# One VectorE addition placed ahead of a subtraction in the second feed-forward, and the second head's activation moved from the mixer's start to its second unit

## The reference

```python
# mixer: one head after the other (8 heads, key width 128)
f = lbf + (1.0 - lbf) * jax.nn.sigmoid(f_logit.astype(f32))
k = 1.0 - f
logf = jnp.log(f)
qf = jax.nn.silu(q.astype(f32))
...
ac = jnp.cumsum(to_chunks(logf, A_KDIM), axis=3)
# per chunk: scores from q, k and exp of differences of ac, then the output and the state S
...
# feed-forward
u, v = jnp.split(z @ w_up[l], 2, axis=-1)
u = causal_dwconv(u, conv_w[l], conv_b[l])
h = h + (jax.nn.silu(u) * v) @ w_down[l]
```

## Time and profile before

| | us |
|---|---|
| median of 3 runs | 3150.68 |
| lowest and highest | 3145.3, 3151.42 |
| the profiled execution | 3153.7 |
| its span, first to last instruction | 3151.9 |
| second mixer, slots 0 to 31 | 1563 to 2165 |
| second feed-forward, turns with down sums | 2486 to 3056 |

### The profile page before, as it was taken

How to read it: one execution, slowest core, us unless ns; L and a number is a source line. 1 busy time by engine, 2 the same in 40 slices (tenths; PEclk the granted TensorE clock), 3 DMA queues, 4 the chain that set the end, 5 groups by cost and what they waited for, 6 DMA issues and landing times. The chain is left out here.

```text
span 3151.9 us, 52430 instructions
## 1 busy us (share of the span) xinstructions
PE 3046.3 (97%) x22212; PEld 2640.2 (84%) x22212; DVE 1520.4 (48%) x2121; ACT 1044.3 (33%) x1503; POOL 751.7 (24%) x634
## 2 busy tenths in 40 slices
PE   7999999799999999999999999999999999999999
PEld 6778888678788888888998999898978888888887
DVE  6898664543433333446365656663432333333333
ACT  3133444333212222133445555554322112111112
POOL 0003321312211222121243434432221122221121
PEclk9999999899999999999999999999999999999999
DMA  3111000311111111123111010112421111111111
GB/s 120 49 47 28 3 3 3 139 63 61 61 40 40 47 47 47 61 81 103 41 48 48 28 48 28 48 46 97 134 97 41 61 47 47 47 57 43 40 41 74
DMA packets 198609, 173.28 MB, mean 55 GB/s; under 512 B 8829, under 2 KB 180437, under 8 KB 198037
## 3 DMA queue, kind: packets, MB, share of 16 engines
q1 hardware_dynamic: 191509, 162.01, 16.2%
q10 hardware_dynamic: 6912, 8.52, 0.8%
HBM read 149.41 MB, written 21.10 MB: 54 GB/s over the span
## 5 line engine op out<-in xcount | busy, mean ns | idle before, releaser
L2142 POOL TENSOR_TENSOR ffn_w_lo<-ffn_raw,ffn_w_hi 128x1024 fp32r<-128x1024 f32 x86 | 207.1, 2409 | 1052.8 <-ACT ffn_w_hi L2302 794.6
L2163 PE MATMUL ffn_out<-blk_hi,ffn_w_hi 128*128 128x512 f32 (+1 forms) x1584 | 446.1, 369 | 3.9 <-DVE blk_lo L1948 2.5
L2163 PE MATMUL ffn_out<-blk_hi,ffn_w_lo 128*128 128x512 f32 (+1 forms) x1584 | 445.6, 369 | 0.0
L2163 PE MATMUL ffn_out<-blk_lo,ffn_w_hi 128*128 128x512 f32 (+1 forms) x1584 | 445.1, 369 | 0.0
L3223 PE MATMUL mix_e<-blk_hi,mix_w_hi 128*128 128x348 f32 (+1 forms) x1056 | 349.0, 331 | 5.6 <-DVE blk_lo L2421 2.9
L3223 PE MATMUL mix_e<-blk_lo,mix_w_hi 128*128 128x348 f32 (+1 forms) x1056 | 342.0, 324 | 0.0
L3223 PE MATMUL mix_e<-blk_hi,mix_w_lo 128*128 128x348 f32 (+1 forms) x1056 | 341.0, 323 | 0.0
L2163 PEld LDWEIGHTS ffn_out<-blk_hi,ffn_w_hi 128*128 128x128 f32 x1584 | 288.7, 189 | 49.5 <-issue 4.9
L2163 PEld LDWEIGHTS ffn_out<-blk_lo,ffn_w_hi 128*128 128x128 f32 x1584 | 288.7, 189 | 44.0
L2163 PEld LDWEIGHTS ffn_out<-blk_hi,ffn_w_lo 128*128 128x128 f32 x1584 | 288.3, 189 | 44.4
L2302 ACT ACTIVATE ffn_w_hi<-ffn_raw 128x1024 fp32r<-128x1024 f32 x44 | 46.7, 1061 | 740.5 <-PE ffn_out L2163 740.5
(11 more groups left out here) (387 smaller groups left out, 5419.1 us busy)
## 6 DMA issues: line engine op xcount, KB each, us to landing
ffn_raw<-ffn_up SPq DMA_DIRECT2D x44, 512.0 KB, 3.8
mix_raw<-w_in SPq DMA_DIRECT2D x44, 512.0 KB, 3.8
ffn_raw<-w_up SPq DMA_DIRECT2D x44, 512.0 KB, 3.8
ffn_d_raw<-ffn_down SPq DMA_DIRECT2D x11, 1024.0 KB, 5.7
ffn_d_raw<-w_down SPq DMA_DIRECT2D x11, 1024.0 KB, 5.8
proj_w_raw<-w_in_first SPq DMA_DIRECT2D x19, 512.0 KB, 3.8
branch_gates<-proj SPq DMA_DIRECT2D x16, 520.0 KB, 4.7
wout_raw<-w_out SPq DMA_DIRECT2D x16, 512.0 KB, 4.2
```

The source lines that it names most:

```text
L2142: G.by(nc.gpsimd.tensor_tensor(w_lo[i % 2][:], raw[i % 2][:], w_hi[i % 2][:], ALU.subtract), f"lo{i}")
L2163: mm = nc.tensor.matmul(o, a[i % 2][:, k, :], b[:, k, first:first + n], start=k == 0 and part == 0, stop=k == KD - 1 and part == 2)
```

## The change

In the second feed-forward, DVE's addition of down0 (`drain(0, 1)`) is placed between `hidden(1)` and `hidden_lo(1)`; the other fifteen stay behind `hidden_lo(1)`. The list of names is changed to the same order. In the mixer, `activate_head(1)` is taken from ahead of slot 0 and put into slot 1, after the last exponentials of unit 2 and before the evacuation of dense piece 32. No instruction is added or removed, apart from register work. Lines of the changed kernel are shifted by 2 or 3.

```diff
--- before.py
+++ after.py
@@ -2013,7 +2013,9 @@
                 dve_names += [f"tapa{2 * q + e}", f"tapb{2 * q + e}"]
         dve_names += [f"hid{q}", f"hid_lo{q}"]
     dve_names += DOWN
-    if not second:
+    if second:
+        dve_names = dve_names[:dve_names.index("hid_lo1")] + ["down0", "hid_lo1"] + DOWN[1:]
+    else:
         dve_names = dve_names[:dve_names.index("tapa3")] + ["tapa3", "down0", "tapb3", "down1", "down2", "hid1", "down3",
                                                             "down4", "hid_lo1"] + DOWN[5:]
     pe_names = [f"up{i}" for i in range(4)] + DOWN
@@ -2475,8 +2477,9 @@
                 if second:
                     taps_of(1)
                     hidden(1)
+                    drain(0, 1)
                     hidden_lo(1)
-                    drain(0, 2 * NT)
+                    drain(1, 2 * NT)
                     return
                 A.wait(dve, g, "y2")
                 tap(2, 1, taps + wide, "tapa2")
@@ -2966,7 +2969,6 @@
             evacuate(25)
             last_level(0)
             evacuate(26)
-            activate_head(1)
             for u in range(slots):
                 more, dense, tiles = u + 1 < slots, pieces_of_slot(u), tiles_of(u)
                 if more:
@@ -2994,6 +2996,8 @@
                     last_level(u + 1)
                 if u and u % 8 == 0:
                     deviation(u // 8 - 1)
+                if u == 1:
+                    activate_head(1)
                 activations(u)
                 for p in dense[2:]:
                     evacuate(p)
```

## The result

| | before | changed |
|---|---|---|
| median (runs) | 3149.22 us (4) | 3127.48 us (4) |
| lowest and highest | 3145.3, 3151.42 | 3124.0, 3132.04 |
| the profiled execution, its span | 3153.7, 3151.9 | 3132.04, 3130.2 |

The ratio of changed to before is 0.9931, with a 95% interval of 0.9919 to 0.9942: 21.7 us less, and between 18.3 and 25.5 by the interval. The forecast was 3131.7 us, 19.0 less, with a range of 3124.5 to 3141.

A forecast was written before the change was run, and what follows sets the result against it. PE, busy 97%, bounds the kernel, so only its waits can be won. Feed-forward 12.2 plus slot 0's 7.2 minus 0.4 in slot 2 gives 19.0 us less: 3131.7 us, 80% range 3124.5 to 3141.

The forecast's parts named there:

- What bounds the kernel: Whole kernel: PE is busy 97% of the span, so time can only be won where PE stands still.
- The moved addition: Second feed-forward, DVE: down0's addition fills the hole before the low part, about 2487.5 to 2488.2, with 0.35 us to spare.
- the choice between 12.2 and 5.6 us: Second feed-forward, nine turns: 12.2 us gained if POOL doesn't hold the moved addition; 5.6 if it does, a rival at 8%.
- Down3 and down4: Second feed-forward: down3's stall of 1.46 us goes, down4 keeps a 0.11 us restart; 1.35 us gained a turn, 12.2 in nine.
- The tie at down4: Second feed-forward: down1's addition ends at 2491.36, down4 is due at 2491.42; no time waited, but a 0.11 us restart probably stays.
- Slot 0: Mixer: the 3.57 us wait vanishes, the keys wait some 0.3, keys to scores take 4.44; 7.2 us gained, lower bound 4.7.
- Slots 1 and 2: Mixer: the block in slot 1 makes ACT 0.9 us late against 0.6 slack in slot 2; PE loses 0.4 us once.
- The rival of a delay that is carried: Mixer, 2%: slot 2 doesn't absorb ACT's delay and 30 later slots wait; 0.9 us costs 12 us, 1.5 gives 3162.
- the rival of a longer switch of tables: Slot 1, 3%: ACT empties 1.28 us before each of two loads, block 7.4 us, PE waits 2.6 more; gain 16.4, 3134.
- The sum: Whole kernel: 12.2 + 7.2 - 0.4 = 19.0 us less, 3131.7 us against the median; the forecast has 73%.
- The clock at slots 8, 16 and 24: Mixer: some 3 us of the range allowed for the clock's fall appearing or vanishing there and for the spread of runs.

The follow-up runs named there:

- Both halves alone: Against the kernel before: only the feed-forward's addition moved, 3139.02 us, ratio 0.996; only head 1's activation moved to slot 1, 3143.56 us, ratio 0.998.
- the longer block: Changed kernel with two more table loads and two 472-column activations ahead of head 1's activation in slot 1: 3136.21 us, ratio 0.996 to the kernel before.
- the repeated pair: Changed kernel and kernel before, both unchanged, once more on another chip: 3129.98 us (ratio 0.9938) and 3151.01 us (ratio 1.0001).
- the experiments for 0.3 and 1 us: Changed kernel with head 1's activation at slot 0's end, 3129.44 us; with two additions ahead of the low part, 3128.44 us; with three, 3130.01 us.

## Why the prediction was right

1. **What bounds the kernel.** PE, and what counts is its idle places and the lower clock behind them. Both halves alone gave what they took out of PE's chain.
2. **The moved addition.** Forecast to start directly behind the gating, to take 0.69 us, and to leave 0.35 us before the low part; the trace has 0.69 and 0.34. That POOL doesn't hold it, the choice between 12.2 and 5.6 us, was right. The Trainium skill (GPSIMD Engine Reference, Specifications) names a collision for VectorE instructions with two SBUF inputs (and for those in a two-port mode, which no run here shows); the trace agrees, 0.69 us for the addition with an operand in PSUM and for the low part 2.21 us beside POOL, 1.26 with an overlap of 0.17 us and 1.22 behind POOL.
3. **Down3 and down4.** The tie at down4 came as forecast, with the restart of 0.11 us and no bracket, and the late weight load shows the reason that the prediction gave. The chain has the sixteen sums in 21.93 us; from the first down matmul to the next up product it was 2509.24 - 2485.92 = 23.32 before and is 2498.52 - 2476.59 = 21.93 now. 1.39 us in this turn and 12.4 in the nine together, for 1.35 and 12.2.
4. **Slot 0.** 7.3 us for 7.2. The keys' wait is 0.36 for 0.3, keys to scores 4.43 for 4.44. One step in it was right with too weak a proof: that PE is at the values at 1567.69 doesn't show dense piece 27 finished when its evacuation was to start, at 1566.95. The trace of before does. Piece 27's last matmul ends at 1566.52:

```profile
1566.20 0.32 PE L3223 MATMUL mix_e<-blk_hi,mix_w_lo 128*128 128x348 f32 x1
```

   More than half of the gain is the idle time of 3.57 and part of the 1.55; (13.25 - 5.94) - (3.57 + 1.55 - 0.36) = 2.6 us of it is matmuls that no longer run at the lower clock, and a restart saved.
5. **Slots 1 and 2.** 0.26 us for 0.4, and some luck in it. The delay was 0.62 us and not 0.9: the block started 0.12 us earlier against the scores of slot 1 and took 4.74 us in place of 4.86. The slack was smaller too. The prediction counted 0.6 us from the end of DVE's sum to the outputs, but PE starts them 0.25 to 0.26 us behind that end even when it is waiting, as here and with the longer block, so about 0.35 were free. The two errors nearly cancel, and the restart of 0.11 us isn't seen here. The loss vanishes in the trace with the block at the end of slot 0, and it is paid once, as the longer block shows with sixteen times the loss (4.11 us over 1.33, for 0.26). The rival of a delay that is carried is refuted. Of the rival of a longer switch of tables: in slot 1, behind other work, each activation follows its load directly and the block takes 4.74 us. The Trainium skill (ScalarE: Activation LUTs, What ACT_TABLE_LOAD costs) gives a switch 2.66 us with its drain; the trace has 1.28 us for it here too, and the measurement decides.
6. **The sum.** 12.4 + 7.3 - 0.26 = 19.4 us in the traces, for 19.0. The measured 21.7 of the first comparison holds 2.3 more. The traces put 2.4 us of the profiled pair ahead of slot 0, and the repeated pair, which starts level, has 19.6 us in all: the 2.4 are not the change's. Why the first 690 us vary by 7.7 us with the same instructions is only in part known; the kernels that arrive late had the lower clock for longer, and what decides that stays open.
7. **The clock at slots 8, 16 and 24.** The prediction left some 3 us for it. In all twelve kernels profiled the keys wait 1.17 us at slots 8 and 16 and 1.23 at slot 24. The clock fell behind the wait of slot 8 in five of them and behind that of slot 16 in two, never behind both and never at slot 24; in two it fell near 1984 us instead, behind a wait of 0.8 us for DVE. From the scores of slot 1 to the first down matmul the eleven kernels without the longer block take between 904.0 and 905.8 us, so the clock's chance, that of the falls just behind the mixer included, was worth at most 1.8 us.

Not told apart in the time: the experiments for 0.3 and 1 us. Their effects are read in the traces alone, and the 0.26 us of slot 2 only at their place, since the 1.8 us of chance cover them in any longer stretch.

## What to carry to other kernels

An in-order engine should first do what someone waits for, if its input is there: an addition that frees a bank goes ahead of a low part that nobody needs for many microseconds, and it is free where the engine had a hole anyway. A long block without urgency belongs where the engine next waits for PE at least as long as the block lasts; one release later than the one that it delayed isn't enough, since the next release takes over the wait whole, and between two uses of one table it costs a load more. Price a stall by the distance of the matmuls around it, the restart and the lower clock behind it included, not by its bracket: here 1.46 us for a bracket of 1.20, and 7.3 for 4.8.

## What was unexpected of the hardware

- The same low part on DVE takes 2.21 us when it starts 1.12 us before POOL's subtraction ends, 1.26 when it starts 0.17 before, and 1.22 behind it, while an addition with one operand in PSUM takes 0.69 in the midst of POOL's 2.40.
- An additional use of a table costs 1.28 us or nothing, depending on which function stood before and which comes next.
- Identical code ahead of both edits reached the same matmul between 685.6 and 693.3 us in twelve profiles on several chips: 7.7 us of spread, more than the whole gain of slot 0.
